# A hybrid decoder step: the rounded half of each weight unit comes by a second DMA instead of a GpSimd multiplication

## The reference, cut to what matters

```python
mix @ w_out                                        # output projection
xp = _residual(xp, yp, g_post_mix[l], mp[2])       # x + gate * rmsnorm(y)
hp = _modulate(xp, g_pre_ffn[l], mp[3], mp[4])     # rmsnorm(x) * (1 + scale) + shift

def _conv_ffn(h, buf, w_up, conv_w, conv_b, w_down):
    L = h.shape[1]
    up = jnp.concatenate([buf, h @ w_up], axis=1)
    y = conv_b
    for i in range(CONV_W):
        y = y + conv_w[i] * up[:, i:i + L]
    a, b = jnp.split(y, 2, axis=-1)
    return (jax.nn.gelu(a) * b) @ w_down, up[:, L:]
```

## Time and profile before

| | us |
|---|---|
| median of three runs | 3570.78 |
| the profiled execution | 3569.11 |
| its span, first to last instruction | 3567.2 |
| PE busy | 3049.9 (85%) |
| GpSimd (POOL) busy | 1112.5 (31%) |
| DVE busy | 1547.0 (43%) |
| POOL line 908 (`f_hi`), 162 times | 318.1 |
| POOL line 911 (`f_lo`), 162 times | 420.8 |

### The profile page before, as it was taken

How to read it: one execution, slowest core, us unless ns; L and a number is a source line. 1 busy time by engine, 2 the same in 40 slices (tenths; PEclk the granted TensorE clock), 3 DMA queues, 4 the chain that set the end, 5 groups by cost and what they waited for, 6 DMA issues and landing times. The chain is left out here.

```text
span 3567.2 us, 52370 instructions
## 1 busy us (share of the span) xinstructions
PE 3049.9 (85%) x19700; PEld 2808.7 (79%) x19700; DVE 1547.0 (43%) x1988; ACT 882.5 (25%) x1751; POOL 1112.5 (31%) x605
## 2 busy tenths in 40 slices
PE   4699986788688999999984999677397999999996
PEld 2688874444588999999984989566296999999996
DVE  2144113555466444344446000286628544434445
ACT  4111111333323222212215111243213222122212
POOL 1212100000563343324321223173263433333340
PEclk9899997899799999999997999889798999999998
DMA  4354543765332111111103212111232111111113
GB/s 162 119 175 170 175 134 123 285 236 185 108 104 68 42 47 47 41 41 47 47 22 114 71 56 71 61 49 36 96 125 101 54 43 45 38 50 47 41 41 102
DMA packets 155051, 322.91 MB, mean 91 GB/s; under 512 B 12754, under 2 KB 86451, under 8 KB 145987
## 3 DMA queue, kind: packets, MB, share of 16 engines
q1 hardware_dynamic: 118178, 244.31, 20.6%
q10 hardware_dynamic: 36768, 77.21, 6.2%
HBM read 275.84 MB, written 45.64 MB: 90 GB/s over the span
## 5 line engine op out<-in xcount | busy, mean ns | idle before, releaser
L908 POOL TENSOR_TENSOR f_hi<-f_st,ones 128x1024 fp32r<-128x1024 f32 x162 | 318.1, 1964 | 1048.2 <-PE f_acc L520 1032.1
L520 PE MATMUL f_acc<-m_hi,f_hi 128*128 128x352 f32 x1248 | 410.9, 329 | 43.4 <-DVE f_lo L495 39.1
L520 PE MATMUL f_acc<-h_hi,f_hi 128*128 128x352 f32 x1248 | 411.4, 330 | 27.0 <-DVE f_lo L495 20.7
L911 POOL TENSOR_TENSOR f_lo<-f_st,f_hi 128x1024 fp32r<-128x1024 f32 x162 | 420.8, 2598 | 12.7
L1261 DVE TENSOR_TENSOR y<-y,f_acc 128x1056 f32<-128x1056 f32 x176 | 218.7, 1252 | 449.0 <-PE f_acc L520 449.0
L520 PE MATMUL f_acc<-h_hi,f_lo 128*128 128x352 f32 x1248 | 407.9, 327 | 0.0
L520 PE MATMUL f_acc<-m_hi,f_lo 128*128 128x352 f32 x1248 | 407.3, 326 | 0.0
L520 PE MATMUL f_acc<-h_lo,f_hi 128*128 128x352 f32 x1248 | 405.5, 325 | 0.0
L520 PE MATMUL f_acc<-m_lo,f_hi 128*128 128x352 f32 x1248 | 404.9, 324 | 0.0
L520 PE MATMUL f_acc<-f_ghi,f_hi 128*128 128x352 f32 x1056 | 346.0, 328 | 31.3 <-issue 20.2
L520 PE MATMUL f_acc<-f_ghi,f_lo 128*128 128x352 f32 x1056 | 343.7, 326 | 0.0
(11 more groups left out here) (357 smaller groups left out, 6109.0 us busy)
## 6 DMA issues: line engine op xcount, KB each, us to landing
f_st<-w_ffn SPq DMA_DIRECT2D x132, 512.0 KB, 3.5
kt<-cache_k SPq DMA_DIRECT2D x128, 256.0 KB, 5.0
att_vt<-cache_v SPq DMA_DIRECT2D x128, 256.0 KB, 5.7
y<-w_ada ACTq DMA_DIRECT2D x20, 1024.0 KB, 5.1
qkv_ada_w<-w_ada ACTq DMA_DIRECT2D x20, 1024.0 KB, 5.3
y<-w_qkv SPq DMA_DIRECT2D x10, 1024.0 KB, 5.9
x<-y ACTq DMA_DIRECT2D x6, 1408.0 KB, 5.5
n_x<-x SPq DMA_DIRECT2D x12, 704.0 KB, 7.9
```

The costliest lines, as they stand in the source:

```text
L520: last = nc.tensor.matmul(out, a(kk), b(kk), start=(n == 0), stop=(n == 3 * nk - 1))
L908: nc.gpsimd.tensor_tensor(hi[u % NSL][:], st[u % 2][:], bc(g.ones[:, 0:1], [P, UW]), ALU.mult).then_inc(pc, 1)
L911: nc.gpsimd.tensor_tensor(lo[u % NSL][:], st[u % 2][:], hi[u % NSL][:].bitcast(F32), ALU.subtract).then_inc(made, 1)
```

## The change

`split` no longer multiplies. GpSimd waits until the slot is free, starts a DMA of its own from the weights in HBM into `f_hi` (float32 in memory, float32r in the tile, so the transfer converts), waits for `landed` and for that transfer, and subtracts. SP's load of `f_st` stays.

```diff
+        hi_landed = [k.sem(f"hi_landed{z}") for z in range(NSL)]
...
             def split(i, u):
+                pool.wait_ge(used, i * 6 + (u + 1))
+                pool.dma_start(hi[u % NSL][:], w_out[u % KB] if u < OUT else w[i * 6 + (u - OUT)])\
+                    .then_inc(hi_landed[u % NSL], 16)
                 pool.wait_ge(landed[u % 2], i * 48 + 16 * (u // 2 + 1))
-                pool.wait_ge(used, i * 6 + (u + 1))
-                nc.gpsimd.tensor_tensor(hi[u % NSL][:], st[u % 2][:], bc(g.ones[:, 0:1], [P, UW]),
-                                        ALU.mult).then_inc(pc, 1)
-                pool.wait_ge(pc, i * 6 + (u + 1))
+                pool.wait_ge(hi_landed[u % NSL], i * 32 + 16 * (u // NSL + (0 if u % NSL == 0 else 1)))
                 nc.gpsimd.tensor_tensor(lo[u % NSL][:], st[u % 2][:], hi[u % NSL][:].bitcast(F32),
                                         ALU.subtract).then_inc(made, 1)
```

## The result

The changed kernel takes 3597.28 us (median of 5 runs, 3593.99 to 3606.37) against 3570.78 us before: a ratio of 1.0077, 95% interval 1.0066 to 1.0089. It is 26.5 us slower; 3561 was forecast. The profiled execution has a span of 3595.5 us against 3567.2, 28.3 us more.

What follows compares the result with a forecast made beforehand. PE, busy 85%, was taken to bound the kernel, with GpSimd costing it time through blocked DVE. Two layers x -5.0 = -10.0 us took the profiled 3569.1 to 3559.1, or 3560.8 at the runs' median; whole range 3530 to 3656.

Steps and rivals of the forecast that it cites:

- The period: GpSimd's time per unit, working without pause: transfer 5.1, gap 0.1, subtraction 2.5, together 7.7 us against 4.78 before.
- c: Time in which GpSimd makes one unit without pause; forecast 7.7 us, ends 5.8 and 11.9, nothing gained at 8.0.
- The projection: Output projection, units 1 to 18: PE waits for GpSimd's units instead of DVE and ACT; -5.0 us per layer.
- The loads of x: Projection: loads of x behind unit 4's load slow the transfer beside them, 7.5 for 3.5 us, once per layer.
- d: Projection: delay added to GpSimd's path by the loads of x, 4.0 us, once per layer.
- DVE's relief: DVE blocked 2.5 of 7.7 us instead of always; four L1164 under 6 us instead of 8.93; worth nothing in the loop.
- The FFN's loop: FFN up and down units: PE waits for nothing, the longer period fits the slot's 11.67 us; no change in time.
- cover of 4.0 us: FFN's loop: GpSimd's room between its 7.7 us per unit and the shortest slot time of 11.67 us.
- The slower rival: GpSimd's queue paces projection units 1 to 16: 16 us per layer per us of c beyond 8.0; chance of slower 0.42.
- The memset's case: DVE's memset of y delays unit 19's transfer 3.0 us per layer: +6, 3567 us; chance 0.13 together with no change.
- Traffic: Second read of the weights adds 85 MB; the loop's DMA share is 0.14, so twice that does not bind.
- signs of being wrong: Transfers over 5.5 us beside SP's load, PE waiting for GpSimd in units 2 to 7, loop below 674 of 680 us.

Runs made afterwards that it cites:

- e3_dma_wait_taps: The full change plus a wait in the FFN's loop, holding GpSimd's subtraction at the down product's start until DVE's taps are done: 3556.56 us, 0.9963 of before.
- e5_mul_delay: The kernel before, no GpSimd transfers, with two memsets between multiplication and subtraction in the FFN's units to delay the subtraction: 3597.19 us, ratio 1.0074.
- e1_proj_dma: The kernel before, with only units 1 to 15 (the projection) made by transfer and the FFN's units still by multiplication: 3569.96 us, ratio 0.9996.
- e4_traffic: The kernel before, plus a 512 KB GpSimd transfer per FFN unit into a tile nothing reads: 3571.66 us, ratio 1.0001.
- e9_mul_hold: The kernel before, all by multiplication, plus a wait making the unit at the down product's start only after DVE's taps: 3571.03 us, ratio 0.9999.

## Why the prediction was wrong

**The period.** Right. Landing 5.1 us beside SP's load was forecast and measured, the subtraction 2.4 for 2.5, c = 7.5 for 7.7. The estimate of 3.2 us by the Trainium skill (DMA: Bandwidth & Descriptors, Anatomy of one DMA — SWDGE (gpsimd) path), 2.0 us plus the bytes by 436 GB/s, was too low here: the trace has 4.0 us with no load beside it, 5.1 with one.

**The projection.** Right in kind, a few us off. Waits for DVE were to become waits for GpSimd, for -5.0 us per layer; the ledger has +1.85 and -3.68. The loads of x cost nearly what was set: the transfer beside them, unit 4's, took 8.4 and 8.5 us instead of 5.1, 3.3 and 3.4 more where d was 4.0. The term that was mis-sized is the subtraction, taken at 2.5 us for all units. Its median is 2.4, but DVE holds it up as it holds up DVE. Unit 14 of the first layer, GpSimd and then DVE:

```profile
1052.68 5.54 POOL L912 TENSOR_TENSOR f_lo<-f_st,f_hi 128x1024 fp32r<-128x1024 f32 x1 [6.03 <-DMA f_hi<-w_out_ab]
```
```profile
1051.53 4.05 DVE L1184 SCALAR_TENSOR_TENSOR f_xs<-y,mod,f_rstd 128x352 f32<-128x352 f32 x8
```

It took 5.54 us, 3.1 more than the median, beside eight operations of DVE in a row without a pause, and PE waited 6.06 us for it. Unit 15 of the second layer took 5.55 beside `low_part`. In the first layer, besides, the transfers of units 2, 14 and 15 took 7.8, 6.6 and 7.0 us to the subtraction's start, for 5.1. Unit 15's ran beside ACT's load of the last third of x (issued at 1055.62); for the other two the reason stays open. `e3_dma_wait_taps` has the same instructions up to the loop, and there unit 2's took 5.0 us and the projection part 162.90 us instead of 166.24, so the first layer's +1.85 is in part chance. DVE's relief came as forecast: four L1165 take 2.07 and 4.16 us, where four L1164 took 8.93 and, the next four, 7.88. One reading in the prediction was too broad: of the eight L1201 that took 11.78 us, only the last four ran beside GpSimd, 2.2 to 2.7 us each; the first four took 0.57.

**The FFN's loop.** This step failed: "DVE's relief is worth nothing here, since PE waits for nothing", with a cover of 4.0 us for GpSimd. The cover was right; GpSimd was never late. But PE did wait there, 0.56 us an iteration for DVE's addition, so DVE had no slack at that point. The 5.6 us by which 674.4 us falls short of 680 are these ten waits; they stood in the row, and the prediction did not look them up. The step asked only whether the longer period fits into the slot's time. It did not ask what the subtraction, moved from 1.97 to 4.1 us behind the release, would now run beside. In its place the runs showed a tap of 3.25 us for 1.33, waits of 1.33 and 0.72 us an iteration, and an iteration of 72.50 us for 70.74. The rule of the Trainium skill that I had used for the gain (SBUF — State Buffer, Who interferes with whom) holds for the loss too, and `e5_mul_delay` shows it with no transfer from GpSimd in the kernel.

**The rivals.** The slower rival named another place and price: 3597 by that rival would have needed c = 8.8. That the time lay among its prices is luck, and `e1_proj_dma` shows that its place cost nothing. The memset's case did not occur: unit 19's transfer started at 1113.99 in the middle of DVE's memset and its subtraction at 1117.88, 3.9 us later, no more than in the quiet loop (4.1). Traffic was rightly set to nothing (`e4_traffic`). Of the signs of being wrong, two came: PE waited 2.37 us for unit 4 of the first layer, and the loop's stretch fell to 659.4 of 680 us.

**The size.** 20 iterations x 1.76 = 35 us, less 1.8 in the projection, less some 3 on the way into the loop, less 2.2 ahead of the stages: 28 us of span, and 26.5 us between the medians.

## What to carry to other kernels

When a change makes an operation on GpSimd later, hiding it in its own slack is half of the question; the other half is which two-input operations of DVE it now runs beside, and whether PE waits for those. A wait of half a us in a steady loop marks a place without slack: look it up before calling the loop PE-bound. Where the collision can't be avoided by moving work, a wait can hold back the uncritical side; here it cost nothing by itself (`e9_mul_hold`) and turned +0.8% into -0.4%, and taking the transfer only where DVE's chain is what PE waits for gave -0.5% with three transfers per layer.

## What the runs showed of the hardware

- A converting 512 KB transfer from GpSimd's queue (float32 to float32r) lands in 4.0 us alone and 5.1 us beside another of 512 KB, against 3.6 us for SP's plain one; it holds GpSimd for 0.57 us. How much of the difference is the converting and how much the queue was not separated.
- 122 such transfers beside the FFN (`e4_traffic`) cost nothing measurable.
- DVE's addition with one input in PSUM took 1.25 us beside GpSimd's memsets, its multiplication or its subtraction alike. The taps, with both inputs in SBUF, were held up by the subtraction: from 1.33 to 1.48 (before), 2.98 (`e5_mul_delay`) and 3.25 us (the change), and each time the tap ended 1.13 or 1.14 us behind the subtraction.
- It goes the other way too: beside a row of such DVE operations without a pause, a subtraction of 2.4 us took 5.54.
- A memset of GpSimd held up no such DVE operation. In `e5_mul_delay` one and the same L1192 took 2.21 us beside the multiplication (1060.77), 0.57 and 0.58 beside the two memsets (1062.91 and 1063.41), and 2.68 beside the subtraction (1064.40).
